# Half of a second weight tile is loaded and multiplied between two halves of a modulation

## What is computed

```python
mod = cond @ w_ada[l] + b_ada[l]
shift1, scale1, gate1, shift2, scale2, gate2 = ...
hmix = _rmsnorm(x, norm_mix_w[l]) * (1.0 + scale1) + shift1
proj = hmix @ w_in[l]
cb, cc, cx, nq, nk, nv, gqkv, gz, ga, gb = jnp.split(proj, split_at, axis=-1)
```

## Time and profile before

| | us |
|---|---|
| median of three executions | 1603.94 |
| lowest and highest of them | 1598.68 and 1604.2 |
| span of the profiled execution | 1604.5 |
| TensorE busy in it | 1447.4 (90%) |
| VectorE busy in it | 789.2 (49%) |
| stretch that the change rewrites, from the start of the span | 24.6 to 65.6 |

### The profile page before, as it was taken

How to read it: one execution, slowest core, us unless ns; L and a number is a source line. 1 busy time by engine, 2 the same in 40 slices (tenths; PEclk the granted TensorE clock), 3 DMA queues, 4 the chain that set the end, 5 groups by cost and what they waited for, 6 DMA issues and landing times.

```text
span 1604.5 us, 16976 instructions
## 1 busy us (share of the span) xinstructions
PE 1447.4 (90%) x6276; PEld 782.9 (49%) x6276; DVE 789.2 (49%) x1867; ACT 291.9 (18%) x705; POOL 312.2 (19%) x291
## 2 busy tenths in 40 slices
PE   6999999799999999999999988988797877787778
PEld 4877875644444444444546755555442333333333
DVE  2256645423232332322533677555687676767544
ACT  1422431100000000000143342122122121212111
POOL 0001010100000000000000043453564444444441
PEclk9999999899999999999999998999999898999999
DMA  9642456599999999999626087999999999999996
GB/s 364 271 157 93 158 193 263 219 402 425 426 426 426 425 426 426 425 426 426 290 76 221 32 337 296 400 421 390 405 405 421 421 421 422 422 421 421 421 421 283
DMA packets 63827, 550.58 MB, mean 343 GB/s; under 512 B 9088, under 2 KB 9376, under 8 KB 10752
## 3 DMA queue, kind: packets, MB, share of 16 engines
q1 hardware_dynamic: 25792, 277.47, 42.2%
q0 software_dynamic: 37952, 271.99, 41.6%
HBM read 548.39 MB, written 1.05 MB: 342 GB/s over the span
## 4 chain that ended last, share of the span: by engine, by line
PE 62%; DMA 26%; DVE 5%; issue 4%; ACT 2%; POOL 1%; SPq 0%; DVEq 0%; POOLq 0%; ACTq 0%
PE ps L1871 13%; DMA ring<-peer_uv_d,work 13%; PE ps L1640 11%; PE ps L1213 7%; DMA ring<-expert_w_d 5%; PE ps L1681 5%; PE ps L1719 5%; DMA work<-peer_uv_d,work 4%; PE ps L1338 4%; PE ps L1207 3%; PE ps L1588 3%; PE ps L1651 3%; DMA work<-expert_w_d 2%; PE ps L1497 2%; PE ps L1221 1%
## 5 line engine op out<-in xcount | busy, mean ns | idle before, releaser
L1871 PE MATMUL ps<-ring,work 128*128 128x512 f32 x720 | 342.8, 625 | 63.8 <-ACT work L1150 63.6
L2971 DVE CUSTOM_DVE_ANT_0 ring<-ring,work 128x1024 f32<-128x1024 f32 x180 | 219.8, 1223 | 113.4 <-DMA ring<-peer_uv_d,work 111.4
L1871 PEld LDWEIGHTS ps<-ring,work 128*128 128x128 f32 x720 | 141.5, 201 | 250.2 <-issue 171.5
L2027 POOL DMA_INDIRECT ring<-peer_uv_d,work x180 | 202.5, 1125 | 227.8 <-PE ps L1871 167.9
L1640 PE MATMUL ps<-ring,work 128*64 128x512 f32 x768 | 168.1, 592 | 4.0 <-DMA ring<-expert_w_d 3.2
L1150 ACT ACTIVATE work<-consts_sb,work 128x128 f32<-128x128 f32 x256 | 85.7, 392 | 257.0 <-DVE work L2980 236.2
L1213 PE MATMUL ps<-ring,hT 128*128 128x512 f32 (+1 forms) x288 | 119.3, 570 | 0.8 <-ACT hT L1014 0.8
L1640 PEld LDWEIGHTS ps<-ring,work 128*64 128x64 f32 x768 | 56.2, 137 | 112.8 <-issue 111.8
L2531 DVE TENSOR_TENSOR work<-work,ps 128x512 f32<-128x512 f32 x16 | 11.0, 687 | 191.3 <-PE ps L1640 191.3
L1871 PE MATMUL ps<-work 128*128 128x512 f32 x160 | 78.0, 632 | 21.9 <-ACT work L1150 21.8
L2003 POOL DMA_DIRECT2D mod<-subkeys_d x1 | 0.6, 552 | 480.8 <-DVEq L2590 480.8
(11 more groups left out here) (430 smaller groups left out, 1836.0 us busy)
## 6 DMA issues: line engine op xcount, KB each, us to landing
ring<-expert_w_d SPq DMA_DIRECT2D x72, 2048.0 KB, 19.9
work<-expert_w_d SPq DMA_DIRECT2D x36, 1024.0 KB, 19.9
ring<-w_ada_d SPq DMA_DIRECT2D x12, 2048.0 KB, 8.5
ring<-w_in_d SPq DMA_DIRECT2D x12, 2048.0 KB, 25.4
consts_sb<-expert_w_d SPq DMA_DIRECT2D x12, 1024.0 KB, 21.1
ring<-w_out_d SPq DMA_DIRECT2D x4, 2048.0 KB, 8.5
ring<-peer_w_query_d SPq DMA_DIRECT2D x4, 2048.0 KB, 8.3
ring<-peer_uv_d,work POOLq DMA_INDIRECT x180, 22.5
```

The costliest lines, as they stand in the source:

```text
L1871: last = pe.matmul(ps[V_BANK[t] + n][:, :], diag[:, i % 4, :], v_row(i)[:, n * 512:(n + 1) * 512], start=(i % (16 * PH) == 0), stop=(i % ( ...
L2027: pool.indirect_dma_start(out=uv_rows(i), out_offset=None, in_=io["peer_uv"], in_offset=bass.IndirectOffsetOnAxis(ap=idx[:, s, k:k + 1], a ...
L2971: dve.tensor_tensor_reduce(out=u_row(i), in0=u_row(i), in1=h_tok[:, i // (16 * PH), :], scale=1.0, scalar=0.0, op0=ALU.mult, op1=ALU.add, ...
```

## The change

The low half of the query tile is loaded right behind the low half of the key tile, ahead of `ada1` and `ada3`, and its sixteen matmuls are put between and around `modulation(1)` and `modulation(3)`, where the fourth key chunk also comes earlier. The high half of the query tile is loaded where the whole tile was. In the later stage only the high-half matmuls of the query tile remain; the 16 gate matmuls stay there, two behind each of the eight query matmuls of `q0`. The jobs `q0`, `gab`, `q1` move to banks 4, 3 and 5, and the banks of all later jobs but the last two are renumbered by three places, their order kept.

```diff
     jobs = [..., ("k0", 6, "D"), ("k1", 7, "D"),
+            ("q0", 4, "D"), ("gab", 3, "D"), ("q1", 5, "D")]
...
-    for name in ("q0", "gab", "q1", "v0", "v1"):
+    for name in ("v0", "v1"):
         add(name, "D")
...
+        q_half_landed = sem("q_half_landed")
...
             half_tile(2, 0, half_landed)
+            half_tile(5, 0, q_half_landed)
             for i in range(3, 5):
                 head_tile(i)
             half_tile(2, 1, head_landed[4])
-            head_tile(5)
+            half_tile(5, 1, head_landed[5])
...
-            def key_chunk(bank, c0, at, g):
+            q_tile = ring[:, 5, :].rearrange("p (k n) -> p k n", n=512)
+
+            def key_chunk(bank, c0, at, g, tile=k_tile):
                 for k in range(4 * g, 4 * g + 4):
-                    last = pe.matmul(ps[bank][:, at:at + T], k_tile[:, k, c0:c0 + P], hT[:, k, :],
+                    last = pe.matmul(ps[bank][:, at:at + T], tile[:, k, c0:c0 + P], hT[:, k, :],
...
             key_chunk(6, P, T, 0)
-            modulation(1)
             evacuated("xT3")
             key_chunk(7, 2 * P, 0, 0)
+            key_chunk(7, 3 * P, T, 0)
+            pe.wait_ge(q_half_landed, 16)
+            evacuated("xT0")
+            key_chunk(4, 0, 0, 0, q_tile)
+            modulation(1)
+            key_chunk(4, P, T, 0, q_tile)
+            evacuated("xT1")
+            key_chunk(5, 2 * P, 0, 0, q_tile)
             modulation(3)
-            key_chunk(7, 3 * P, T, 0)
+            key_chunk(5, 3 * P, T, 0, q_tile)
             columns(1)
             warm(5)
...
-            evacuated(head_before("gab"))
             pe.wait_ge(in_tail, 16)
             for c in range(2):
                 for k in range(KC):
-                    last = pe.matmul(b[:, c * T:(c + 1) * T], wt[:, k, c * P:(c + 1) * P], hT[:, k, :],
-                                     start=(k == 0), stop=(k == KC - 1))
+                    if k % 2 == 0:
+                        r = 4 + k // 2
+                        last = pe.matmul(b[:, c * T:(c + 1) * T], wt[:, r, c * P:(c + 1) * P], hT[:, r, :],
+                                         start=False, stop=(r == KC - 1), skip_group_check=True)
                     side = pe.matmul(gates[:, 16 * c:16 * c + 16], hT[:, k, c * P:(c + 1) * P], tail_w[:, k, 0:16],
                                      start=(k == 0), stop=(k == KC - 1))
...
-            two_chunks("q1", wt, 256)
+            b = hbank("q1")
+            assert b is ps[5]
+            key_chunk(5, 2 * P, 0, 1, q_tile)
+            hfull(key_chunk(5, 3 * P, T, 1, q_tile))
```

More of the change, by code:

```diff
@@ L120, in head_jobs @@
     jobs = [("xT0", 4, "D"), ("xT1", 5, "D"), ("xT2", 6, "A"), ("xT3", 7, "A"), ("ada0", 0, "D"), ("ada2", 1, "D"),
-            ("col0", 2, "D"), ("ada1", 0, "D"), ("ada3", 1, "D"), ("col1", 2, "D"), ("k0", 6, "D"), ("k1", 7, "D")]
+            ("col0", 2, "D"), ("ada1", 0, "D"), ("ada3", 1, "D"), ("col1", 2, "D"), ("k0", 6, "D"), ("k1", 7, "D"),
+            ("q0", 4, "D"), ("gab", 3, "D"), ("q1", 5, "D")]
     n = [0]
```

## The result

The changed kernel took 1608.95 us (median of nine executions, 1606.97 to 1614.70), the kernel before 1603.03 (nine, 1598.68 to 1605.50). The ratio is 1.0044, 95% interval 1.0030 to 1.0058: some 7 us slower (the two medians alone lie 5.9 us apart), clear of noise and outside the predicted range of 1598 to 1608.

A forecast was written before the change was run, and what follows sets the result against it. TensorE was taken to bound the rewritten stage; +6.94 - 6.94 + 0.1 (gates) - 0.04 (`ada3`) + 0 (clock) = +0.1 us on 1604.5 gave 1604.6, or 1604.0 for the median, range 1598 to 1608.

The forecast's parts named there:

- The renumbering of the later banks: Banks of the jobs behind the moved work: every distance stays at eight jobs, so it was costed at nothing.
- From `gc` on nothing of the order changes: Everything after VectorE takes `gc` at 98.10 us: order unchanged, so the shift was taken through unchanged.
- the sum of +0.1: Whole kernel: all terms added gave +0.1 us on 1604.5, which is 1604.6 for the profiled execution.
- something large further on: The 1500 us of later work: a shift multiplied either way, 10 us either side; chance 0.12, half on each side.
- Matmuls moved, +6.94 and -6.94: Sixteen query matmuls of 0.434 us added around the modulations, sixteen removed from `q0` and `q1`: 6.94 us each way.
- Gates: Gate matmuls in `q0`, every second now behind another gate: 0.22 us each before, eight cost +0.1 us in all.
- Clock: Behind `columns(1)`: the drop to 0.51 of the clock comes again 6.94 us later, no gain and no loss.
- the rival's price: No clock drop behind `columns(1)`: gain 1.7 us, so 1602.3, with `gc` at 96.5; chance 0.19.
- first reading: Whole kernel: TensorE is busy for 1447 of 1604.5 us and its clock is nearly everywhere the full one.
- Transfers: SP's queue: query half lands at 23.5, `ada1` 28.4, `ada3` 34.5, all before they are wanted; at most 0.04 us gained.
- ScalarE as the bound: At `lk0`'s wait for four squares: ScalarE's backlog moves the whole 6.94, TensorE loses 2.2 us, so 1606.2; chance 0.09.
- two new waits for banks: `lq0` for `q0` and `lq1` for `q1`: they ask for VectorE's side taps, which are ahead of the squares.

The follow-up runs named there:

- old banks: The changed kernel with the jobs from `v0` on back in the banks of the kernel before, moved work kept; 1602.48 us, ratio 0.9994.
- groups turned: The changed kernel with the four groups of the output projection's first half reordered, the one in bank 0 last; 1602.52 us, ratio 1.0004.
- new banks: The kernel before with only the bank counter changed, so jobs from `v0` on have the changed kernel's banks; 1613.55 us, ratio 1.0064.
- `w11` first: The kernel before, banks kept, with the output projection's group `w11`, whose bank 3 held `bc7`, put first; 1613.55 us, ratio 1.0071.
- wait filled: The changed kernel with 24 warming matmuls on constants put before the output projection's wait for `bc7`; 1608.24 us, ratio 1.0040.

## Why the prediction was wrong

The step that failed is one sentence, "The renumbering of the later banks keeps every distance at eight jobs, so I cost it at nothing." It is true inside the rotating part of the head's list and false at its end. There the MID jobs take fixed banks, and what they wait for is whichever head job stands last in each. It could have been costed from the trace of before: TensorE starts the line at 250.97, `bc7` is taken at 256.99 + 0.69 = 257.7, so a first group that has to wait for it starts 6.7 us later. Measured: 6.85, and 2.8 more behind it, 2.0 of them on the line that ran at half clock. The premise "From `gc` on nothing of the order changes, and I take the shift through unchanged" and the sum of +0.1 fell with it. The rival "something large further on" had the right region and no mechanism, and at 0.06 too small a chance.

Against that, the rest of the steps:

*Matmuls moved, +6.94 and -6.94: right.* `columns(1)` begins at 43.25 in the chain (42.97 predicted), the second half of the key tile at 46.73 (46.5); counted from the stage's first line, 6.79 us were added. From the query matmuls to the end of the value tile 6.92 us were removed (58.76 + 20.82 - 48.37 before, 64.38 + 13.81 - 53.90 after). With the old banks the ratio is 0.9994.

*Gates: right, and the +0.1 for them was nothing.* A query matmul with two gates takes 0.53 + 0.35 = 0.88 us, so a gate is (0.88 - 0.434) / 2 = 0.22, what it was in a pair. That this is the price of its weight load was argued only.

*Clock: wrong for this execution, and the rival's price right.* The drop did not come, and `gc` was taken at 96.72 where the rival had 96.5. The change can't be given the credit (see below): that the rival came true in this trace was luck. The prediction's first reading, a clock that is nearly everywhere the full one, rests on the clock line of the page of the kernel before, which has 9 (90% or more) in 36 of its 40 slices and 8 in four.

*Transfers: right.* The query half landed at 23.8, `ada1` at 28.7, `ada3` at about 35.1, against 23.5, 28.4 and 34.5; issue and landing give them as before, the rows for the two modulation tiles being

```profile
ring<-w_ada_d SPq DMA_DIRECT2D x1, 2048.0 KB, 23.2
...
ring<-w_ada_d SPq DMA_DIRECT2D x1, 2048.0 KB, 29.1
```

with issues at 5.48 and about 6.0. `gdn_conv_w` was issued until 8.44 + 26.91 = 35.35, 1.5 us later than before (2.45 estimated; that a full queue holds the issue was argued and no run shows it), and the value tile landed at 48.2 (49.4).

```profile
8.44 26.91 SPq L746 DMA_DIRECT2D small<-gdn_conv_w_d  x1
```

*ScalarE as the bound: right that it is not.* The square of `q1` ended at 75.3 and TensorE wanted it at 78.0. It moved by 0.6 us and not by the 3.5 that the prediction took. The prediction also named only two new waits for banks: `lk1` now waits for `gab`, too, and no wait of TensorE for it shows in the trace.

```profile
74.64 0.63 ACT L862 ACTIVATE ring<-work 128x512 f32<-128x512 f32 x1
...
78.03 3.60 PE L1329 MATMUL ps<-ring,consts_sb 128*128 128x512 f32 x8
```

## What to carry to other kernels

When jobs rotate through banks or buffers, a renumbering can keep all distances within the list and still change what meets at its end: write down, for each buffer, the last user of the old list and the first of the new, and compare when each is released and wanted. Put the job that is taken last into the buffer that is wanted last; here the same 6.7 us was free or paid by that alone. And moving matmuls between two places where the engine is busy saved no time here, so an edit like this is judged by its side effects, which can lie far from its lines.

## What the runs showed of the hardware

The clock drop behind `columns(1)` is not set by TensorE's order in this stage alone. The kernel with the groups turned has TensorE's order of the changed kernel in this stage, and the profiled executions differ (the stretch from 36 to 50 us, first the changed kernel, then the turned groups; the clock is the third number from the end):

```profile
36.00:50.00 14.00, 13.43 (x81) 10.54 (x81) 2.73 (x8) 0.60 (x1) 0.00 (x0) 1.00 0.87 321
```

```profile
36.00:50.00 14.00, 13.43 (x74) 10.30 (x73) 2.22 (x8) 0.60 (x1) 0.00 (x0) 0.88 0.93 344
```

The same holds for two kernels with the order of before, 0.88 in the one with new banks and 1.00 in the one with `w11` first. Of the profiles with the order of the change, two have the drop (groups turned, wait filled) and two don't (changed, old banks). Where it came, the second half of the key tile took 8.74 to 8.86 us, elsewhere 7.17, so it is worth 1.6 to 1.7 us in an execution and can't be credited to an edit from one profile. The Trainium skill says in "TensorE: Matmul & The Clock Gate" (Part 1, "What's actually happening") that the window over which activity is judged runs freely and doesn't restart with the kernel. These profiles fit that, 1.00 and 0.88 for one order, but none of them shows the window itself. The slow line behind the 6.68 us wait, on the other hand, was there in all three profiles that had this wait unfilled: 15.92, 15.74 and 16.02 us instead of 13.90.
